# Sixteen weight tiles spaced unevenly against the activations, and one small input loaded later

## What is computed

```
u = rmsnorm(h);  proj = u @ w_in                       # 2048 x 10240
ya = dilated attention(12 heads) @ w_branch_a          # 512 x 2048
yb = stick-breaking attention(4 heads) @ w_branch_b    # 512 x 2048
h += rmsnorm((sigmoid(ga)*ya + sigmoid(gb)*yb) @ w_out)
up = causal_conv3(rmsnorm(h) @ w_up)                   # 2048 x 11264
h += rmsnorm((gelu(gate)*value) @ w_down)              # 5632 x 2048
h += sigmoid(h @ w_ple_gate) * (p @ w_ple_in)          # p: 256 tokens x 256
# second block
proj = rmsnorm(h) @ w_in_2 + b                         # 2048 x 5888
attention(16 heads), diagonal state space (32 groups x 64), w_glu_2
h += (gates * branches) @ w_out_2
h += (val * gelu(conv3(gate))) @ w_down_2;  out = rmsnorm(h)
```

## Time and profile before

| | us |
|---|---|
| median of 2 runs (2675.67 to 2676.21) | 2675.94 |
| the profiled execution, its own time | 2679.38 |
| its span in the trace | 2677.6 |
| TensorE busy in it | 2646.9 |
| VectorE busy | 1833.7 |
| ScalarE busy | 1295.2 |
| GpSimd busy | 249.0 |

### The profile page before, as it was taken

How to read it: one execution, slowest core, us unless ns; L and a number is a source line. 1 busy time by engine, 2 the same in 40 slices (tenths; PEclk the granted TensorE clock), 3 DMA queues, 4 the chain that set the end, 5 groups by cost and what they waited for, 6 DMA issues and landing times.

```text
span 2677.6 us, 54944 instructions
## 1 busy us (share of the span) xinstructions
PE 2646.9 (99%) x21426; PEld 2574.6 (96%) x21426; DVE 1833.7 (68%) x2313; ACT 1295.2 (48%) x1592; POOL 249.0 (9%) x206
## 2 busy tenths in 40 slices
PE   9999999999999999999999999999999999999998
PEld 9999999998999999999999999999988888889998
DVE  6455555747888888864467999767577777775444
ACT  5334455345344444444455566554455555554342
POOL 1000000030000000001101665300100000000000
PEclk9999999999999999999999999999999999999999
DMA  7665555564555555566656555556655565556654
GB/s 257 192 199 173 151 164 181 166 213 149 176 195 195 194 189 196 187 200 200 192 170 199 174 162 157 156 182 206 191 183 194 191 192 191 189 188 198 196 190 141
DMA packets 137804, 496.69 MB, mean 185 GB/s; under 512 B 15424, under 2 KB 15424, under 8 KB 137536
## 3 DMA queue, kind: packets, MB, share of 16 engines
q1 hardware_dynamic: 137520, 494.20, 57.7%
q10 hardware_dynamic: 144, 0.52, 0.1%
HBM read 492.57 MB, written 2.10 MB: 185 GB/s over the span
## 4 chain that ended last, share of the span: by engine, by line
PE 89%; DVE 6%; DVEq 2%; ACT 1%; issue 1%; DMA 1%; ACTq 0%; SPq 0%
PE twin L442 87%; DVE w_lo L1003 2%; PE ps_o L442 1%; PE ps_n L442 1%; DVE act_x L1042 1%; PE ps_t L442 0%; ACT w_hi L691 0%; DMA hT<-in_xT 0%; DMA w_raw<-in_w_in 0%; ACT act_x L757 0%; DVE hT L1067 0%; DVE pr L1330 0%; DVE rstd L1026 0%; DVEq L1320 0%; DVE hT L1563 0%
## 5 line engine op out<-in xcount | busy, mean ns | idle before, releaser
L1003 DVE TENSOR_TENSOR w_lo<-w_raw,w_hi 128x1024 fp32r<-128x1024 f32 x928 | 1133.2, 1235 | 693.6 <-ACT w_hi L691 691.2
L691 ACT ACTIVATE w_hi<-w_raw 128x1024 fp32r<-128x1024 f32 x928 | 976.3, 1055 | 1161.8 <-PE twin L442 1027.6
L442 PE MATMUL twin<-act_x,w_hi 128*128 128x256 f32 (+1 forms) x9664 | 1395.2, 296 | 8.7 <-ACT act_x L757 5.5
L442 PEld LDWEIGHTS twin<-act_x,w_hi 128*128 128x128 f32 x9664 | 1239.1, 189 | 55.1 <-issue 8.7
L442 PE MATMUL twin<-act_x,w_lo 128*128 128x256 f32 x5536 | 745.8, 278 | 3.5 <-DVE w_lo L1003 3.5
L442 PEld LDWEIGHTS twin<-act_x,w_lo 128*128 128x128 f32 x5536 | 697.1, 188 | 18.9 <-DVE w_lo L1003 4.1
L442 PE MATMUL twin<-f_x,w_hi 128*128 128x256 f32 x2816 | 348.0, 277 | 0.0
L442 PEld LDWEIGHTS twin<-f_x,w_hi 128*128 128x128 f32 x2816 | 332.3, 188 | 0.0
L442 PE MATMUL twin<-f_x,w_lo 128*128 128x256 f32 x1408 | 188.4, 277 | 0.0
L442 PEld LDWEIGHTS twin<-f_x,w_lo 128*128 128x128 f32 x1408 | 172.7, 188 | 0.0
L1575 POOL COPY tab<-tab 128x512 f32<-128x512 f32 x5 | 5.2, 1049 | 1750.1 <-ACT tab L710 1750.1
(11 more groups left out here) (207 smaller groups left out, 1463.0 us busy)
## 6 DMA issues: line engine op xcount, KB each, us to landing
w_raw<-in_w_up SPq DMA_DIRECT2D x352, 512.0 KB, 4.2
w_raw<-in_w_in SPq DMA_DIRECT2D x252, 512.0 KB, 3.9
w_raw<-in_w_down SPq DMA_DIRECT2D x176, 512.0 KB, 4.2
w_raw<-in_w_out SPq DMA_DIRECT2D x64, 512.0 KB, 4.4
w_raw<-in_w_ple_gate SPq DMA_DIRECT2D x32, 512.0 KB, 4.5
w_raw<-in_w_branch_attn SPq DMA_DIRECT2D x16, 512.0 KB, 3.6
w_raw<-in_w_branch_a SPq DMA_DIRECT2D x8, 512.0 KB, 4.1
w_raw<-in_w_branch_b SPq DMA_DIRECT2D x8, 512.0 KB, 3.5
```

The lines of the kernel that those rows point to most:

```text
L442: return pe.matmul(o, l, r, start=start, stop=stop, skip_group_check=True)
L691: act.activation(w_hi[:, k, 0:n, :], w_raw[:, k, 0:n, :], ACT.Copy).then_inc(hi_ready, 1)
L1003: dve.tensor_tensor(w_lo[:, k, 0:n, :], w_raw[:, k, 0:n, :], w_hi[:, k, 0:n, :].bitcast(F32), ALU.subtract).then_inc(lo_ready, 1)
```

## The change

The ring's tiles of `w_hi` and `w_lo` get 16 floats (64 bytes) of room behind each tile and 4 floats (16 bytes) more behind each slot of 4 tiles; the two skips ahead of them become zero; the skip before the stages' buffers becomes 56 floats. `pT` is gone: p is loaded into `val_y`, behind a wait of SyncE at piece 8 of down, and split beside piece 14. The reads and writes of the ring take the same elements as before.

```diff
+ROW = GROUP + 16
+SLOT = PIECE_KT * ROW + 4
+HI_OFF, LO_OFF, STAGE_OFF = (0, 0, 56)
-        sb("before_w_hi", [P, 48])
-        w_hi = sb("w_hi", [P, RING, PIECE_KT, GROUP], F32R)
-        sb("before_w_lo", [P, 32])
-        w_lo = sb("w_lo", [P, RING, PIECE_KT, GROUP], F32R)
+        w_hi_ring = sb("w_hi", [P, RING * SLOT], F32R)
+        w_lo_ring = sb("w_lo", [P, RING * SLOT], F32R)
+        w_hi, w_lo = ([ring[:, k * SLOT:k * SLOT + PIECE_KT * ROW].rearrange("p (t g) -> p t g", g=ROW) for k in range(RING)]
+                      for ring in (w_hi_ring, w_lo_ring))
-        pT = sb("pT", [P, 2, TOK])
-        sb("before_stages", [P, 8])
+            sb("before_stages", [P, STAGE_OFF])
-                        if st is st_mix and at == 0:
-                            sp.dma_start(pT[:, :, :], a["pT"]).then_inc(p_landed, 16)
+                        if st is st_down and isinstance(i, int) and i == 0 and at == 8:
+                            sp.wait_ge(f_ready, 22)
+                            sp.dma_start(val_y[:, :, :], a["pT"]).then_inc(p_landed, 16)
...
-                    act.activation(w_hi[:, k, 0:n, :], w_raw[:, k, 0:n, :], ACT.Copy).then_inc(hi_ready, 1)
+                    act.activation(w_hi[k][:, 0:n, 0:GROUP], w_raw[:, k, 0:n, :], ACT.Copy).then_inc(hi_ready, 1)
...
-                if n == 4:
+                if n == 14:
                     dve.wait_ge(p_landed, 16)
                     dve.drain()
-                    split(pT[:, :, :], p_hi[:, :, :], p_lo[:, :, :]).then_inc(split_ready, 1)
+                    split(val_y[:, :, :], p_hi[:, :, :], p_lo[:, :, :]).then_inc(split_ready, 1)
```

More of the change, by code:

```diff
@@ L156, in build @@
         w_raw = sb("w_raw", [P, RING, PIECE_KT, GROUP])
-        sb("before_w_hi", [P, 48])
-        w_hi = sb("w_hi", [P, RING, PIECE_KT, GROUP], F32R)
-        sb("before_w_lo", [P, 32])
-        w_lo = sb("w_lo", [P, RING, PIECE_KT, GROUP], F32R)
+        if HI_OFF:
+            sb("before_w_hi", [P, HI_OFF])
+        w_hi_ring = sb("w_hi", [P, RING * SLOT], F32R)
+        if LO_OFF:
+            sb("before_w_lo", [P, LO_OFF])
+        w_lo_ring = sb("w_lo", [P, RING * SLOT], F32R)
+        w_hi, w_lo = ([ring[:, k * SLOT:k * SLOT + PIECE_KT * ROW].rearrange("p (t g) -> p t g", g=ROW) for k in range(RING)]
+                      for ring in (w_hi_ring, w_lo_ring))
         tab = sb("tab", [P, TAB_COLS])
         par = sb("par", [P, PAR_COLS])
-        pT = sb("pT", [P, 2, TOK])
         rstd = sb("rstd", [P, TOK])
@@ L168, in build @@
         ssm, ssm_i = sb("ssm", [P, 30, STATE_TILES]), sb("ssm_i", [P, STATE_TILES], I32)
-        sb("before_stages", [P, 8])
+        if STAGE_OFF:
+            sb("before_stages", [P, STAGE_OFF])
         half_bias = lambda j: half_b[:, j:j + 1]
@@ L467, in body @@
                                 for c in range(2):
-                                    mm(ps[:, c * TOK:(c + 1) * TOK], w_hi[:, k, t, c * P:(c + 1) * P],
+                                    mm(ps[:, c * TOK:(c + 1) * TOK], w_hi[k][:, t, c * P:(c + 1) * P],
                                        xh[:, x0 + j * PIECE_KT + t, :], j == 0 and t == 0 and c == 0, False)
@@ L472, in body @@
                                 for c in range(2):
-                                    mm(ps[:, c * TOK:(c + 1) * TOK], w_lo[:, k, t, c * P:(c + 1) * P],
+                                    mm(ps[:, c * TOK:(c + 1) * TOK], w_lo[k][:, t, c * P:(c + 1) * P],
                                        xh[:, x0 + j * PIECE_KT + t, :], False, False)
@@ L477, in body @@
                                 for c in range(2):
-                                    last = mm(ps[:, c * TOK:(c + 1) * TOK], w_hi[:, k, t, c * P:(c + 1) * P],
+                                    last = mm(ps[:, c * TOK:(c + 1) * TOK], w_hi[k][:, t, c * P:(c + 1) * P],
                                               xl[:, x0 + j * PIECE_KT + t, :], False, j == st.pieces[s] - 1 and t == n - 1)
@@ L490, in body @@
                                 o = ps[:, c * TOK:(c + 1) * TOK]
-                                w = w_hi[:, k, t, c * P:(c + 1) * P]
+                                w = w_hi[k][:, t, c * P:(c + 1) * P]
                                 if st.halves:
@@ L502, in body @@
                                 o = halves_of(st, s)[0][:, c, :] if st.halves else ps[:, c * TOK:(c + 1) * TOK]
-                                last = mm(o, w_lo[:, k, t, c * P:(c + 1) * P],
+                                last = mm(o, w_lo[k][:, t, c * P:(c + 1) * P],
                                           xh[:, x, :], False, j == st.pieces[s] - 1 and t == n - 1)
@@ L1002, in piece @@
                     dve.wait_ge(hi_ready, q + 1)
-                    dve.tensor_tensor(w_lo[:, k, 0:n, :], w_raw[:, k, 0:n, :], w_hi[:, k, 0:n, :].bitcast(F32),
+                    dve.tensor_tensor(w_lo[k][:, 0:n, 0:GROUP], w_raw[:, k, 0:n, :], w_hi[k][:, 0:n, 0:GROUP].bitcast(F32),
                                       ALU.subtract).then_inc(lo_ready, 1)
```

## The result

The changed kernel takes 2748.93 us (median of 2, 2748.64 to 2749.21) against 2675.94: 1.0273 of before, 95% interval [1.0229, 1.0317], so slower. Its profiled span is 2746.8 us, 69.2 more than before.

What follows compares the result with a forecast made beforehand. TensorE was taken to bound the kernel, busy 2646.9 of 2677.6 us. Terms 0 - 5 + 0 + 0 = -5 us from 2679.4 gave 2674.4, and 2671 us after 3.4 us for the runs' median; range 2661 to 2708.

Steps and rivals of the forecast that it cites:

- Part 1: Steady spacing of the ring's matmuls, 113.3 ns: would neither fall nor rise, taken as 0, upper end +77 us.
- The upper bound of 4.4 ns: Ring matmuls: the slow spacing of mix for every one, 85 us less roughly 8 already paid, +77.
- The first rival: Stages free of slow spacing, up, down and down2 above all: 117.5 ns spreads, up to 2753 us; chance 0.22.
- The rival's sign: Next profile: 850 to 880 matmuls in a window of down, mean durations 280 instead of 276 ns, some slots only.
- Part 2: Slow stretches in mix, in2 and up2: changing distances end them sooner, -5 of 13 us there to be had.
- The ports: TensorE's reads: addresses have no part, slow stretches follow pauses; no change, 2676 us within 2; chance 0.20.
- The floor: Steady ring matmuls: 113.3 ns holds a collision and falls by 4.4 ns, 85 us off, 2591 us; chance 0.04.
- Parts 3 and 4: The ring's two copies over gaps, and p's later load and split: 0 each; far ends +22, and 1.1 plus 5.6 us.

Runs made afterwards that it cites:

- b_tile64: Changed kernel with 64 bytes behind each tile, nothing more per slot, both rings at a multiple of 64 bytes: 2734.73 us.
- m: Changed kernel with 128 bytes behind each w_hi tile, w_lo even, starts at 192 and 320 bytes as before the change: 1.0008 of before.
- j: Changed kernel with ring addresses at 64 modulo 128 as before the change, and act_x moved by 64 bytes: 2747.93 us.
- a_p_only: Changed kernel with the rings put back as before the change, leaving only p's later load and split: 1.0001 of before.
- d to g: Changed kernel with even rings (tiles 1024 bytes apart) at 96, 0, 32 and 96 modulo 128: 2721.13, 2780.22, 2759.16 and 2763.43 us.
- n: Changed kernel with even rings at distance 48 modulo 128 from act_x and the stages' buffers alike: 2767.26 us.
- o: Changed kernel with even rings at distance 80 modulo 128 from act_x and the stages' buffers alike: 2753.76 us.
- e_at0: Changed kernel with even rings, tiles 1024 bytes apart, all at 0 modulo 128 bytes: 2780.22 us.
- i_act64_w0: Changed kernel with even rings; act_x and rings both moved by 64 bytes from the kernel before, weights at 0 modulo 128: 2727.56 us.
- r: As i_act64_w0, but w_lo a further 128 bytes off: 2721.99 us.

## Why the prediction was wrong

**The step that failed** is Part 1, "Can it rise?", and in it the word "fair". It took 0 for the steady spacing on the strength of eight distances that all showed 113 ns. They were one. The 464 bytes came from adding up sizes without the rounding of starts; the built program has 512, so `f_x` lies at the same four distances as `act_x`, and all four, 192, 320, 704 and 832, are 64 modulo 128. What looked like eight free points was one, the only free one of the six tried. The runs put a number in its place: 4 to 7 ns a matmul at each of the five other distances and 4.7 in the changed kernel, where the text took 0. The upper bound of 4.4 ns, kept for the range's working, was the right one, and its case had only 0.09 for over 2%.

**The sum.** The first rival had the mechanism, that some distances slow the ring, and the price: 4.4 ns for 19360 matmuls less 8 us gave +77, and 2753 us; measured 2748.9. Its terms measured: 118.0 - 113.3 = 4.7 ns for a matmul in the steady windows, +73.5 us outside up2, +8.4 in up2 (1.8 of it at the 512-column matmuls, which the 77 left out), -12.0 for the longer gaps (which nothing in the text priced). That 4.4 ns, taken from the slow spacing of mix, came so near is in part luck: it is the second rate of distance 64, 117.8 ns, while the changed kernel's 118.0 ns comes from distances mixed, and an even ring at 0 has 120.0.

The rival's sign, 850 to 880 matmuls in a window of down, came at its edge, 850. It was to show in some slots only, and all four slots had it, with 117.5 to 118.5 ns.

Its point of decision was drawn wrongly: "Some of the sixteen distances" near 0 modulo 512, a quarter of the tiles. Modulo 128 the sixteen are 0, 16, 32, ... 112, each twice in each ring. Only the two at 64 could be free, and they were not. 16 and 112 were not tried alone. The six that were average (120.0 + 118.3 + 119.3 + 113.3 + 118.2 + 118.7) / 6 = 118.0 ns, which is what the changed kernel has, but that is no explanation: its matmuls at 64 take 117.7 ns and not 113.3. In b_tile64 the average of 0 and 64 would be 116.7 ns, and it has 117.2.

**Part 2**, -5 us for stretches of longer spacing cut short by changing distances, is refuted for the change, where nothing is left of 113.3 ns. The idea in it may be half right: with uneven tiles at multiples of 128 (m) slow gaps outside up2 were 5.1 us less, in one trace of each. What the forecast didn't see is that up2 gives it back, 5.8 us.

**The ports.** By the Trainium skill, "SBUF — State Buffer", section "Who interferes with whom", the two read ports of TensorE are independent and PE never waits on anyone, and the rival built on it had 0.20. The measurement differs: in j moving the moving operand's buffer by 64 bytes, with the weights at the same place modulo 128, takes a matmul from 113.3 to 120.0 ns in up and leaves it at 113.3 in down. That it is a collision of the two reads in SBUF is the reading that fits; no run shows the ports themselves.

**The floor.** Sixteen placements gave no steady stage under 113.3 ns, so that rival is out for all that was tried. The argument against it by the 512-column matmul stands: in all these kernels one takes 229 to 234 ns in up2. At distance 0 it takes 230.1 ns, against 229.4 in the kernel before, while a 256-column one takes 120.0 against 113.3. The formula N / 2.4 + 2.5 ns is given by the Trainium skill, "TensorE: Matmul & The Clock Gate", section "Back-to-back issue gap", for an isolated matmul and not for a stream with weight loads, so it says little of this floor. The prediction's 113.0 and 112.8 ns come from window counts; from the starts they are 113.3, and nothing rests on the difference.

**Parts 3 and 4** held. The copies take 1239 and 1059 ns, unchanged. p's load was issued at 1123.8 us in a_p_only, in the stretch named, with no wait of SyncE for `f_ready` in the profile, and no cost can be seen: 1.0001 [0.9990, 1.0013]. The timeline of VectorE after has the split beside piece 14:

```profile
1179.88 0.66 DVE L1030 CAST p_x<-val_y 128x512 fp32r<-128x512 f32 x1
1180.62 0.81 DVE L1032 TENSOR_TENSOR p_x<-val_y,p_x 128x512 fp32r<-128x512 f32 x1
```

0.35 us longer than in the earlier trace rows, and hidden all the same.

## What to carry to other kernels

Where weight loads and moving operands stream from SBUF side by side, choose both buffers' addresses together, modulo 128 bytes, and keep every tile at the one good distance. Spreading the distances doesn't average a risk away: the tiles that still had the good distance here lost their rate with the others. Take addresses from the built program before calling two places different: rows that agree are evidence only if the variable really varied between them. And when a row shows a second, longer spacing in one place, ask what keeps the rest of the kernel out of it before pricing the rest at zero.

## What the runs showed of the hardware

- With fp32r operands, 256 moving columns and a load of 128 columns for each, the distance modulo 128 bytes between weights and moving tile is worth 113.3 against 117 to 120 ns (before; d to g, j, n, o), and of six values tried only 64 is free; 48 and 80 are not.
- The free rate needs a stretch of loads at 64. With tiles at 0 and 64 in turn (b_tile64) the matmuls at 64 take 117.4 ns.
- 512-column matmuls don't follow this distance: 230.1 ns at 0 (e_at0), 229.4 at 64 in the kernel before and 232.7 at 64 in i_act64_w0.
- The same addresses can run at more than one rate: at 64, 113.3 or 117.8 ns (i, r); at 48, 119.3 or 117.8 (n). In i a pause of 2.48 us stood at the change, and the slower rate held for 3840 matmuls. What selects the rate, and why the modulus is 128, stays open.
- A buffer's start is rounded up to 32 bytes in these programs, so a skip of 208 bytes put the ring at 224.
